# One layer's adaLN vectors as dot products on VectorE instead of products on TensorE, in a four-layer fp32 block

## What is computed

```python
for layer in range(DEPTH):
    mod_l = (jax.nn.silu(c) @ w_ada[layer] + b_ada[layer])[:, None, :]
    mod_c = jax.nn.silu(c_ctx) @ w_ada[layer] + b_ada[layer]
    sh1_l, sc1_l, g1_l, sh2_l, sc2_l, g2_l = jnp.split(mod_l, 6, axis=-1)
    ...
    h_l = modulate(x_l, sh1_l, sc1_l)
    h_c = modulate(x_c, sh1_c, sc1_c)
```

## Time and profile before

| | |
|---|---|
| median of 3 runs | 2009.37 us (2007.9 to 2012.42) |
| profiled execution | 2011.44 us, span 2009.6 us, granted clock 0.995 |
| PE (matmul) busy | 1967.1 us, 98% |
| DVE busy | 1128.8 us, 56% |
| ACT busy | 385.7 us, 19% |
| POOL busy | 14.2 us, 1% |
| DMA | 295.85 MB, mean 147 GB/s; SP's queue 36.8% and POOL's 1.8% of 16 engines |

### The profile page before, as it was taken

How to read it: one execution, slowest core, us unless ns; L and a number is a source line. 1 busy time by engine, 2 the same in 40 slices (tenths; PEclk the granted TensorE clock), 3 DMA queues, 4 the chain that set the end, 5 groups by cost and what they waited for, 6 DMA issues and landing times.

```text
span 2009.6 us, 26366 instructions
## 1 busy us (share of the span) xinstructions
PE 1967.1 (98%) x11574; PEld 1388.9 (69%) x11574; DVE 1128.8 (56%) x1583; ACT 385.7 (19%) x801; POOL 14.2 (1%) x28
## 2 busy tenths in 40 slices
PE   8998999999999999999999999999999999999998
PEld 7775658954594698447854558888874466659973
DVE  4554757654365466444426835455555665736776
ACT  3313101000314101012113722111110212321110
POOL 0000000000000000000000000000000000000000
PEclk9999999999999999999999999999999999999999
DMA  6647764453443244532241011222224453124442
GB/s 250 258 159 309 286 284 184 168 204 152 167 168 126 105 172 167 215 133 90 84 188 63 1 43 42 91 99 99 89 84 156 186 204 147 43 84 168 168 155 96
DMA packets 23329, 295.85 MB, mean 147 GB/s; under 512 B 2784, under 2 KB 3200, under 8 KB 5168
## 3 DMA queue, kind: packets, MB, share of 16 engines
q1 hardware_dynamic: 21024, 280.70, 36.8%
q0 software_dynamic: 2192, 13.47, 1.8%
HBM read 293.08 MB, written 1.08 MB: 146 GB/s over the span
## 4 chain that ended last, share of the span: by engine, by line
PE 90%; DVE 7%; DMA 1%; ACT 1%; issue 1%; SPq 0%; DVEq 0%; ACTq 0%
PE bank L352 88%; DMA ring<-in_W 1%; PE bank L715 1%; DVE small L884 1%; DVE arena L905 1%; PE bank L808 0%; DVE arena L726 0%; DVE arena L898 0%; DVE arena L669 0%; DVE arena L879 0%; ACT arena L842 0%; DVE arena L625 0%; DVE arena L2693 0%; DVE HT L2565 0%; DVE ADR L1088 0%
## 5 line engine op out<-in xcount | busy, mean ns | idle before, releaser
L352 PE MATMUL bank<-arena 64*64 64x64 f32 (+8 forms) x4548 | 628.9, 318 | 13.3 <-issue 3.5
L352 PEld LDWEIGHTS bank<-arena 128*128 128x128 f32 (+3 forms) x4548 | 433.0, 167 | 194.6 <-issue 155.0
L352 PE MATMUL bank<-HT,ring 128*128 128x128 f32 (+1 forms) x2448 | 408.0, 325 | 4.5 <-DMA ring<-in_W 2.1
L352 PEld LDWEIGHTS bank<-HT,ring 128*128 128x128 f32 x2448 | 362.6, 192 | 44.5 <-issue 9.2
L352 PE MATMUL bank<-ring,arena 128*128 128x512 f32 (+1 forms) x674 | 295.5, 593 | 0.0
L352 PEld LDWEIGHTS bank<-ring,arena 128*128 128x128 f32 (+1 forms) x674 | 126.9, 190 | 155.5 <-issue 155.1
L352 PE MATMUL bank<-ring,HT 128*128 128x512 f32 (+1 forms) x480 | 189.4, 552 | 1.0 <-ACT HT L2063 0.8
L352 PE MATMUL bank<-arena,ring 128*128 128x128 f32 (+4 forms) x1158 | 187.2, 322 | 0.0
L352 PEld LDWEIGHTS bank<-arena,ring 128*128 128x128 f32 (+3 forms) x1158 | 165.4, 189 | 15.1 <-issue 2.0
L352 PEld LDWEIGHTS bank<-ring,HT 128*128 128x128 f32 x480 | 85.4, 190 | 97.8 <-issue 94.6
L724 ACT ACTIVATE arena<-bank 128x512 f32<-128x512 f32 (+2 forms) x97 | 51.8, 566 | 420.6 <-PE bank L352 418.9
(11 more groups left out here) (315 smaller groups left out, 1498.0 us busy)
## 6 DMA issues: line engine op xcount, KB each, us to landing
ring<-in_W SPq DMA_DIRECT2D x118, 2048.0 KB, 7.8
arena<-in_W SPq DMA_DIRECT2D x7, 2048.0 KB, 12.7
ring<-in_W SPq DMA_DIRECT2D x6, 1536.0 KB, 8.7
ring<-in_W SPq DMA_DIRECT2D x4, 1024.0 KB, 9.0
arena<-in_rel POOLq DMA_DIRECT2D x1, 2048.0 KB, 11.1
arena<-in_rpb POOLq DMA_DIRECT2D x1, 2048.0 KB, 9.7
arena<-gate_rows POOLq DMA_DIRECT2D x1, 2048.0 KB, 15.3
X<-in_x SPq DMA_DIRECT2D x2, 512.0 KB, 5.8
```

The lines of the kernel that those rows point to most:

```text
L352: return nc.tensor.matmul(out_, lhsT, rhs, start=start, stop=stop, skip_group_check=True)
```

## The change

The adaLN vectors of layer 0 leave TensorE; those of layer 1 stay, as 12 steps renumbered 0 to 11. On the host the layer-0 weight is turned (`adaT`): column block j, 128 of the 6144 outputs on the partitions with their 1024 weights each, 512 KB. GpSimd loads the two conditions spread to all partitions (`wide`, 1 MB) into the free half of `HT`, ACT takes their Silu in place (`act_wide`), and for each of 48 columns DVE takes two dot products over 1024 elements with `tensor_tensor_reduce`, one for each condition, and writes each sum to its place in `MOD` (`dve_columns`). The column weights come through GpSimd's queue into two buffers of 1024 elements; load j waits until column j - 2 is done. The columns are spread: 4 in eout before DVE's first addition, 1, 1, 1 and 2 behind the up blocks of mlp0, 4, 4, 4 and 3 behind its down chunks' sums, 2 at its end, 2 and 5 in attn, 1, 1, 1, 2 and 4, 4, 2, 0 in mlp1. The bias follows in mlp1 (`dve_mod_columns`); norming and turning the context tokens moves there from down chunk 0 to chunk 3, and layer 0's gate rows from eout to the end of mlp1's down products.

```diff
-    ada = [(f"ada{j // 12}.{j % 12}", 4096) for j in range(24)]
-    plan += ada[0:3] + [("bqkv0", 4096), ada[3], ("bqkv1", 4096), ada[4], ("bqkv2", 4096), ("bab", 256), ("bgate", 4096)] + ada[5:]
+    ada = [(f"ada1.{j}", 4096) for j in range(12)]
+    plan += ada[0:2] + [("bqkv0", 4096), ("bqkv1", 4096), ("bqkv2", 4096), ("bab", 256), ("bgate", 4096)] + ada[2:]
...
+        def dve_scales(i):
+            dve.wait_ge(vector_done, dve.n)
+        def dve_mod():
+            ps = full(dve, "mod1")
+            src = ps[:, 0:P].rearrange("p (m c) -> p m c", m=4)[:, :, 0:24].rearrange("p m (j s) -> p j m s", s=2)
+            bias = C("bada1", 0, 48).rearrange("p (j m) -> p j m", m=4).unsqueeze(3).broadcast_to([P, 12, 4, 2])
+            tt(MOD[:, 1].rearrange("p (j m) s -> p j m s", m=4), src, bias, ALU.add).then_inc(vector_done, dve.one())
+            dve.mark("read mod1")
+            dve_scales(1)
+        WIDE = [HT[:, 4 * s:4 * s + 4, SEQ:512] for s in range(2)]
+        COLW = [arena[:, 25600 + D * b:25600 + D * b + D].rearrange("p (a c) -> p a c", a=4) for b in range(3)]
+        def act_wide():
+            act.wait_ge(loaded["wide"], at("wide in"))
+            activation(HT[:, :, SEQ:512], HT[:, :, SEQ:512], ACT.Silu).then_inc(scalar_done, act.one())
+            act.mark("c wide")
+        def dve_columns(n):
+            dve.wait_ge(scalar_done, at("c wide"))
+            for _ in range(n):
+                j = state["column"]
+                state["column"] += 1
+                w = COLW[j % 2]
+                dve.wait_ge(loaded[f"cols{j % 2}"], at(f"column {j} in"))
+                for s, dst in ((0, COLW[2]), (1, w)):
+                    if s or j:
+                        dve.wait_ge(vector_done, dve.n)
+                    nc.vector.tensor_tensor_reduce(dst, w, WIDE[s], 1.0, 0.0, ALU.mult, ALU.add,
+                                                   MODF[:, 2 * j + s:2 * j + s + 1]).then_inc(vector_done, dve.one())
+                dve.mark(f"column {j}")
+        def dve_mod_columns():
+            dve.wait_ge(vector_done, dve.n)
+            tt(MOD[:, 0], MOD[:, 0], C("bada0", 0, 48).unsqueeze(2).broadcast_to([P, 48, 2]), ALU.add).then_inc(vector_done, dve.one())
+            dve_scales(0)
...
             pe_ada(1)
-            pe_ada(2)
             pe_half_block("bqkv0", "bq", 0, 0)
...
...
                 if k < 3:
-                    pe_ada(k + 2)
                     pe_scores(*(("mrb", AV, R), ("mrk", KF, R))[k - 1])
                     pe_half_block(f"bqkv{k}", "bq", 0, 4 * k)
                 elif k == 3:
                     pe_logits_turned()
                     pe_bgate(0)
-                    pe_ada(5)
                 elif k == 4:
-                    pe_ada(6)
-            pe_ada(8)
-            pe_ada(9)
+                    pe_ada(2)
+            pe_ada(4)
...
             pe_bscores()
-            pe_ada(10)
             pe_chunk_out(0)
-            pe_ada(11)
             for k in range(1, 6):
                 pe_lx("gdn", k, 0, MASKED2, XI2)
                 if k < 4:
                     pe_chunk_in(k)
                 else:
-                    pe_ada(2 * k + 7)
+                    pe_ada(k + 4)
                 pe_xlx("gdn", k, 0, LX2, XT2)
-                if k == 1:
-                    pe_mod(0)
                 if k < 4:
                     pe_chunk_out(k)
-                    pe_ada(11 + k)
-                else:
-                    pe_ada(2 * k + 8)
+                    pe_ada(4 + k)
...
             for c in range(4):
                 if c > 0:
                     pe_bchunk_in(c)
-                pe_ada((19, 20, 22, 23)[c])
+                if c < 2:
+                    pe_ada(10 + c)
                 pe_bchunk_out(c)
-                if c == 1:
-                    pe_ada(21)
...
-            act_gate_rows()
+            act_wide()
+            act_gate_rows(1)
 
         def dve_eout():
-            pass
+            dve_columns(4)
...
-            turns = {(0, 3): lambda: ctx_turn(2, 0), (0, 5): lambda: ctx_turn(2, 1), (0, 7): lambda: ctx_turn(3, 0), (0, 6): lambda: ctx_turn(3, 1)}
+            turns = {(3, 2): lambda: ctx_turn(2, 0), (3, 5): lambda: ctx_turn(2, 1), (3, 7): lambda: ctx_turn(3, 0), (3, 6): lambda: ctx_turn(3, 1)}
             pe_seven(f"down{i}", down_chunks(i), lambda k, t: HH[:, k, t * P:(t + 1) * P], lambda n: M["left"][n % 2], M["right"], lambda n: f"hidden{i}.{n}",
                      bank=lambda j: (b0 + j - 1) % 8, between=turns if i else {})
+            if i:
+                pe_gate_rows(0)
...
             act.wait_ge(vector_done, at(f"up{i}.3 joined"))
             if i:
                 act.wait_ge(loaded["ctx"], at("ctx in"))
+                act.wait_ge(vector_done, at("column 47"))
                 for t in (2, 3):
                     act_rms("mod e", t, four(JKC))
+            act_seven(f"down{i}", M["U"])
+            if i:
+                act.wait_ge(vector_done, at("mod0 ready"))
                 for t in (2, 3):
                     act_turned("mod e", t, mod_scale(0, 0), mod_shift(0, 0), (0, 1))
-            act_seven(f"down{i}", M["U"])
+                act_gate_rows(0)
...
                 if p < 2:
                     dve_left_sums(f"down{i}", p, HH[:, 8 * p:8 * p + 8, :], M["left"][p])
+                dve_columns(1 if p < 3 else 2)
             dve.wait_ge(tensor_done, at(f"up{i} done"))
             for n, (names, kt) in enumerate(down_chunks(i)):
-                if i and n == 0:
-                    for t in (2, 3):
-                        dve_unit("mod e", t, four(XNC[:, t % 2, :]))
                 dve_right_sums(f"down{i}", n, names, kt, M["right"])
                 if 1 <= n < 3:
                     dve_left_sums(f"down{i}", n + 1, HH[:, 8 * n + 8:8 * n + 16, :], M["left"][(n + 1) % 2])
+                dve_columns(((4, 4, 4, 3), (4, 4, 2, 0))[i][n])
+                if i and n == 2:
+                    dve_mod_columns()
+                    for t in (2, 3):
+                        dve_unit("mod e", t, four(XNC[:, t % 2, :]))
             dve_seven(f"down{i}", M["U"], lambda t: f"xt{i} src{t}")
...
             dve.wait_ge(vector_done, dve.n)
+            if i == 0:
+                dve_columns(2)
...
             normed(1, "k3", KB)
+            dve_columns(2)
             dve.wait_ge(loaded["rel"], at("rel"))
             dve_pairs("band", band_steps, PB3)
+            dve_columns(5)
...
+            def rows_out(i):
+                e.wait_ge(scalar_done, at(f"read gate rows{i}"))
+                for j in range(2):
+                    load(f"rows{i}", gate_rows[i, :, j].rearrange("s k c -> k s c"), GROW[i][j])
+                group[f"rows{i}"].mark(f"rows kept{i}")
+
+            def columns(first, end):
+                for j in range(first, end):
+                    if j >= 2:
+                        e.wait_ge(vector_done, at(f"column {j - 2}"))
+                    load(f"cols{j % 2}", COLW[j % 2], T["adaT"][:, j * D:(j + 1) * D].rearrange("p (a c) -> p a c", a=4))
+                    group[f"cols{j % 2}"].mark(f"column {j} in")
+
+            load("wide", HT[:, :, SEQ:512], T["crow"].broadcast_to([P, 2 * D]).rearrange("p (k c) -> p k c", k=KT))
+            group["wide"].mark("wide in")
+            columns(0, 4)
...
             for i in range(2):
+                if i:
+                    e.wait_ge(vector_done, at("k pair joined"))
+                    e.wait_ge(tensor_done, at("k pair p0.4"))
+                    columns(26, 35)
                 after("eout" if i == 0 else "attn")
                 if i == 0:
-                    for n in range(2):
-                        for j in range(2):
-                            load("rows", gate_rows[n, :, j].rearrange("s k c -> k s c"), GROW[n][j])
-                    group["rows"].mark("rows kept")
+                    rows_out(1)
                 load(f"ple{i}", M["pT"], T["pT"][i].rearrange("p (k c) -> p k c", k=2))
                 load(f"ple{i}", M["pg"], row(f"ple{i}"))
                 group[f"ple{i}"].mark(f"p{i}", f"rows ple{i}")
-                if i == 0:
+                if i:
+                    columns(35, 48)
+                    rows_out(0)
+                else:
+                    columns(4, 26)
                     after("mlp0")
...
+            "adaT": np.ascontiguousarray(f["w_ada_2"][0].T.reshape(48, P, D).transpose(1, 0, 2).reshape(P, -1)),
+            "crow": np.concatenate([f["c_2"][0].reshape(-1), f["c_ctx_2"].reshape(-1)])[None, :],
```

108 lines of the change are left out of this document (44 added, 64 removed).

## The result

The changed kernel takes 2030.01 us (median of 4 runs, 2029.15 to 2031.05), the kernel before 2010.39 beside it: a ratio of 1.0101, 95% interval 1.0088 to 1.0114. It is slower by 20 us, or 1%, against a forecast of 2003 with a range of 1991 to 2016. The profiled run took 2030.12 us, its span is 2028.3 us, 18.7 more than before.

A forecast was written before the change was run, and what follows sets the result against it. TensorE was taken as the bound, on the chain for 90% of the span. Mix -20.8, eout +7.6, clock +1.7, first MLP +3.7, second +1.1 made -6.7: 2003 us for the median, range 1991 to 2016.

The forecast's parts named there:

- L: Time of one 512 KB column load over the POOL queue, taken as 4.1 us, ends 3.6 and 6.3.
- that hole: VectorE's idle time in a down chunk of the first MLP: 12.10 us of the 24.03 us period.
- Rival 1: Column loads land late, 6.3 us each; MLPs, eout, attention and clock lose 27.8 us against 20.8: 2016; chance 0.15.
- rival 4: Column reductions on VectorE run at half rate, 5.0 us a column; 86 us lost against 21: 2074; chance 0.03.
- Rival 2: All of it comes off: mix gains 26.5 us, loads take 3.6, no fall of the clock: 1993; chance 0.17.
- Steps 2 to 5: Four removed ada steps in the mix where TensorE runs on without a wait: 7.4 us gained.
- 10 and 11: Two removed ada steps in the mix, before work needing VectorE's mask: 2.9 of 3.7 us gained.
- mod0: Four small matmuls removed from the mixing stage: 1.0 us gained.
- step 9: Removed ada step in the mix that waits 3.22 us for its own weight; both go: 5.1 us gained.
- Steps 16 and 18: Removed ada steps in the mix; 18 is covered by a VectorE wait, two VectorE reads go: 1.4 of 3.7 us.
- Steps 21 to 23: Ada steps in the mix where TensorE and VectorE pass a state; 22 and 23 out: about 3.0 of 5.6 us.
- rival 3: Removed steps were cover: TensorE waits for VectorE instead, clock drops twice; 11.6 won, 14.1 lost: 2012, no change; chance 0.15.

## Why the prediction was wrong

**The step that failed is the price of a load.** "I take L = 4.1, ends 3.6 and 6.3", and from it "four columns at 11.9 fit that hole almost exactly". The median of the 48 loads is 4.1; the loads that DVE waits for in the down chunks took 10.7, 8.2, 6.9 and 6.2. A run of four took 18.6 us in chunk 0 (418.59 to 437.19) and not 11.9. That the first MLP costs 4 us per us of L was right: the four loads took 32.0 us where 4 x 4.1 = 16.4 stood in the sum, 15.6 more, and 3.7 + 15.6 = 19.3 of the 19.8 lost. The value of L was taken from loads that stood elsewhere. The upper end was wrong too, the 6.3 of a row that happened to stand behind others: the end should have been worked out from the burst. An estimate from the 434 GB/s of the windows is 10.9 us for two loads of 2048 KB and one of 512. Those windows were in the trace of before.

**Rival 1 was what happened,** with its mechanism, its place and its evidence ("weight loads follow the sums that stand right ahead of the columns, so both are in flight together"). It got 0.15 because of the mean, "DMA is under half busy in the MLP", and its 2016 was too low by its L of 6.3. The sign given for it, a median over 5.2 us, did not show: the median stayed at 4.1, because most of the 48 loads are not issued into a burst.

**The clock in the MLPs** was not in the sum, and did not have to be. Behind waits of 3.86, 4.40 and 3.83 us the products took 15.70, 12.79 and 17.00 us, where 13.90, 10.46 and 13.90 had been: 7.2 us. Behind 3.52 and 1.12 they took 14.00 and 13.97. By PE's rows the first MLP lost 15.0 us of waits (1.12 + 3.52 + 3.86 + 4.40 + 2.09) and 4.1 of clock, 19.1 of 19.8, the second 6.0 (1.11 + 3.83 + 1.08) and 3.1, 9.1 of 10.4. But behind each of these slow stretches PE waits for DVE again, and DVE in those chunks waits for the loads alone. At the full clock PE would by these rows have waited that much longer.

**The second MLP** was put at 1.1 us. Its two runs of four waited for loads of 11.0 and 8.5 us, 11.3 more than 2 x 4.1. DVE's work of chunks 0 and 1, 21.0 + 23.8 = 44.8 us by the prediction's terms, is 3.3 short of PE's 48.1, so of the 11.3 only 8.0 are lost, with the 1.1 of chunk 0 the 9.1 above.

**The price of a column was right,** 1225 ns and 82 ns against 1.22 and 0.08, and rival 4 is out. The Trainium skill, Vector Engine (DVE) Microarchitecture Reference, section Points that are easy to get wrong, says for `S2S2D2_STT` that two SBUF sources that are not bf16 halve the throughput. The trace doesn't show that for `tensor_tensor_reduce`: 1024 fp32 elements from two SBUF tensors take the same 1.2 us as a plain product. Whether this instruction is of that form no run says.

**Eout came out right within 1.2 us,** +8.1 against +9.3. The left side landed at about 274.3 (issued at 266.61, 7.7 us), 294.7 in the frame of before and not 297.3 (285.84 + 5.2 + 6.0 is 297.0): it did not queue behind the context rows. The four columns took 11.8 us (11.4 forecast), the wait was 5.75, and from turn to turn 2.4 us more (7.60 for 5.21) went to the lower clock, 0 to 3.4 being forecast and 1.7 taken. Rival 2 has 7.2 for eout where the sum gives 7.6 at the same L; neither slip matters. The 1.28 of the table is in the chain and was paid only because the chain was late anyway.

**The first MLP's chunk 0** waited 1.12 us, forecast 1.1, and the second's 1.11. Attention is 0.8 longer, forecast 0.

**The mix was right in its sum, -20.4 against -20.8, and wrong in two terms that cancel.** That it came within 0.4 us is luck: ten profiles of this same mixing stage put it 17.9 to 24.6 us ahead of the one profile of before. Up to the end of the gdn inverse (249.57 before, 224.87 after) the lead is 24.7 us; I had 17.8 there. Steps 2 to 5 gave 8.0 (7.4), 10 and 11 gave 2.9 (2.9), mod0 0.9 (1.0). The place of step 9 gave 8.1, not 5.1: a pause of 2.44 us that followed it has gone too, and products that ran at a lower clock behind the pause gave 1.6 more. Steps 16 and 18, with the waits around them, gave 2.9 (1.4). These rows of before had been there to be read:

```profile
191.36 0.46 PE L352 MATMUL bank<-arena 64*64 64x64 f32 x15 [2.44 <-issue]
...
191.99 4.68 PE L352 MATMUL bank<-KC,arena 128*128 128x128 f32 x48
```

Then 4.3 of the lead are lost again up to eout, where I had 3.0 more to gain. Steps 21 to 23 and step 18 at the end of the inverse were cover, as rival 3 said of them: the wait of 1.49 is 3.13 now, one of 0.52 is 2.38, and the clock falls behind them.

```profile
224.87 2.51 PE L352 MATMUL bank<-X,arena 64*64 64x128 f32 x32 [3.13 <-DVE arena L1058]
...
244.53 12.76 PE L352 MATMUL bank<-arena 128*64 128x128 f32 x56 [2.38 <-DVE arena L1725]
```
```profile
224.00:234.00 10.00, 9.13 (x82) 6.44 (x83) 4.00 (x8) 0.00 (x0) 0.00 (x0) 0.66 0.50 210
...
250.00:262.00 12.00, 11.97 (x56) 9.48 (x56) 6.69 (x11) 1.39 (x3) 0.00 (x0) 0.71 0.01 2
```

A sum that comes out right is no proof of its terms.

## What to carry to other kernels

A load that an engine will wait for is priced by what else is issued in that moment, not by the median of its kind nor by the stage's mean DMA share: look at windows of 2 us around the instruction that frees the big slots, and if the new loads hang on the same instruction, count the whole burst. With n buffers, no more than n items should stand in such a place, or the next one waits for the burst; more buffers made the same work nearly free here, with the loads issued at once or in the gap. Where one engine waits for another again and again, add up the work of the one that never waits for the other: a slower clock or a shorter product on the other side changes nothing. Steps of the matrix engine that stand in front of a wait cost nothing up to that wait's length, and a place may be free of waits only because such a step stands in it.
